# Prompt attention of a hybrid decoder step: TensorE makes a step's value products ahead of the step's transposes

## The reference

```
s = (q_nope @ k_nope^T + q_rope @ k_rope^T) * scale     # kind A
s = q @ k^T * scale                                      # kind B, + log of how many dilations hit the key
p = softmax(mask(s));   o = p @ v
```

## Time and profile before

| | |
|---|---|
| time, median of 3 runs | 1124.61 us (1124.18 to 1126.54) |
| profiled execution, span from first to last instruction | 1121.6 us (median less span: 3.0 us) |
| instructions | 21305 |
| TensorE busy | 98% of the span |
| DVE, ACT, POOL busy | 51%, 42%, 7% |
| stage with the change | about 229 to 333 us of the span |

### The profile page before, as it was taken

One profiled execution on the slowest core, in us unless ns is written; L12 is line 12 of the kernel. 1 busy time (PEld: TensorE's weight loads), 2 busy tenths in 40 slices (PEclk: granted clock), 3 DMA queues, 4 the chain that ended last, 5 costly groups with the idle time before them and its releaser, 6 DMA issues.

```text
span 1121.6 us, 21305 instructions
## 1 busy us (share of the span) xinstructions
PE 1100.4 (98%) x8216; PEld 947.9 (85%) x8216; DVE 572.8 (51%) x999; ACT 465.5 (42%) x812; POOL 81.9 (7%) x124
## 2 busy tenths in 40 slices
PE   9999999989989999999999999999999999999998
PEld 8897888645557777777776999999999999999998
DVE  4321444276657566666657994444423344444554
ACT  4334222355546656565566343333211232223421
POOL 5300011024000000000000220000000000000000
PEclk9999999988989999999999999999999999999999
DMA  7754541325957677788751245645724554562222
GB/s 292 244 190 170 207 141 57 105 113 185 328 171 269 191 246 250 252 270 268 243 180 62 96 150 185 227 151 182 264 88 141 188 206 159 196 221 79 89 87 92
DMA packets 68591, 202.79 MB, mean 181 GB/s; under 512 B 7426, under 2 KB 40195, under 8 KB 67235
## 3 DMA queue, kind: packets, MB, share of 16 engines
q1 hardware_dynamic: 66338, 131.89, 35.9%
q0 software_dynamic: 2176, 69.90, 17.6%
HBM read 196.67 MB, written 72.13 MB: 240 GB/s over the span
## 4 chain that ended last, share of the span: by engine, by line
PE 88%; DVE 5%; issue 3%; ACT 2%; POOL 1%; DMA 0%; SPq 0%; POOLq 0%; DVEq 0%
PE ps L549 52%; PE ps L1346 14%; PE ps L1449 4%; PE ps L1334 2%; PE ps L1323 2%; PE ps L1403 1%; PE ps L1378 1%; PE ps L1397 1%; PE ps L477 1%; PE ps L1308 1%; PE ps L1303 1%; PE ps L449 1%; PE ps L486 1%; POOL xs L726 1%; PE ps L1216 1%
## 5 line engine op out<-in xcount | busy, mean ns | idle before, releaser
L549 PE MATMUL ps<-aHi,wHi 128*128 128x272 f32 x1168 | 245.9, 292 | 0.3 <-DVE aLo L389 0.3
L549 PE MATMUL ps<-aHi,wLo 128*128 128x272 f32 x1168 | 241.6, 288 | 0.0
L549 PE MATMUL ps<-aLo,wHi 128*128 128x272 f32 x1168 | 240.9, 288 | 0.0
L423 ACT ACTIVATE wHi<-ring 128x1024 fp32r<-128x1024 f32 (+3 forms) x102 | 113.4, 1112 | 240.3 <-PE ps L549 213.3
L428 DVE TENSOR_TENSOR wLo<-ring,wHi 128x1024 fp32r<-128x1024 f32 (+3 forms) x102 | 141.1, 1383 | 140.2 <-ACT wHi L423 140.1
L549 PEld LDWEIGHTS ps<-aHi,wHi 128*128 128x128 f32 x1168 | 183.6, 188 | 8.8 <-issue 7.1
L549 PEld LDWEIGHTS ps<-aLo,wHi 128*128 128x128 f32 x1168 | 183.5, 188 | 0.0
L549 PEld LDWEIGHTS ps<-aHi,wLo 128*128 128x128 f32 x1168 | 182.5, 189 | 0.0
L1671 DVE TENSOR_REDUCE ssq<-att 128x8 f32<-128x512 f32 x128 | 87.2, 681 | 83.7 <-ACT att L916 83.7
L916 ACT ACTIVATE att<-ps 128x512 f32<-128x512 f32 x128 | 76.4, 597 | 104.7 <-PE ps L1346 104.1
L1346 PE MATMUL ps<-wkHi,pgHi 128*128 128x512 f32 x256 | 104.2, 407 | 1.5 <-DVE pgLo L1665 1.2
(11 more groups left out here) (266 smaller groups left out, 1476.2 us busy)
## 6 DMA issues: line engine op xcount, KB each, us to landing
out_o_cv<-in_cv POOLq DMA_DIRECT2D x16, 2044.0 KB, 9.1
ring<-in_wgu SPq DMA_DIRECT2D x44, 512.0 KB, 4.3
big<-in_pgt SPq DMA_DIRECT2D x128, 144.0 KB, 2.3
big<-in_pgl SPq DMA_DIRECT2D x128, 128.0 KB, 2.3
kv<-in_ck SPq DMA_DIRECT2D x8, 1792.0 KB, 10.4
ring<-in_win SPq DMA_DIRECT2D x21, 512.0 KB, 4.9
kv<-in_cv SPq DMA_DIRECT2D x8, 1024.0 KB, 5.6
kv<-in_cv SPq DMA_DIRECT2D x24, 256.0 KB, 6.1
```

The costliest lines, as they stand in the source:

```text
L423: nc.scalar.activation(wHi[:, u % 2, 0:width], ring[:, u % 2, 0:width], ACT.Copy).then_inc(w_hi, 1)
L549: ins = nc.tensor.matmul(pair[rows, a, 0:HT], w[:, c], xx[:, k, a * HT:(a + 1) * HT], start=(k == 0 and z == 0), stop=(k == nk - 1 and z = ...
```

## The change

In each step of TensorE's loop the block with the value products of unit n - 3 moves ahead of the block with the transposes of unit n - 2. No instruction is added, removed or changed, and every wait stays with its block. ACT's, DVE's, POOL's and SP's programs stay as they are.

```diff
                 if n < len(units):
                     ...  scores of unit n
-                if n >= LAG_T and n - LAG_T < len(units):
-                    m = n - LAG_T
-                    i = units[m][1]
-                    pe.wait_ge(a_p, m + 1)
-                    if m:
-                        pe.wait_ge(a_tc, m)
-                    for j in range(i + 1):
-                        for z in range(2):
-                            last = pe.transpose(ps[1][:, z, j * P:(j + 1) * P], probs_of(m, z)[:, j * P:(j + 1) * P], cm(C_ID))
-                    last.then_inc(a_t, 1)
                 if n >= LAG_PV:
                     m = n - LAG_PV
                     p, i = units[m]
                     pe.wait_ge(a_tc, m + 1)
                     ...  wait for a_o, value products
                     last.then_inc(a_pv, 1)
+                if n >= LAG_T and n - LAG_T < len(units):
+                    m = n - LAG_T
+                    i = units[m][1]
+                    pe.wait_ge(a_p, m + 1)
+                    if m:
+                        pe.wait_ge(a_tc, m)
+                    for j in range(i + 1):
+                        for z in range(2):
+                            last = pe.transpose(ps[1][:, z, j * P:(j + 1) * P], probs_of(m, z)[:, j * P:(j + 1) * P], cm(C_ID))
+                    last.then_inc(a_t, 1)
```

## The result

The changed kernel takes 1134.5 us (median of 4 executions, 1132.2 to 1137.6) against 1124.8 (median of 4); the ratio is 1.0086 (95% interval 1.0068 to 1.0104). A second round of 6 executions gave 1133.3 and a ratio of 1.0085 (1.0062 to 1.0108). Over all 10 the median is 1133.4; over 101 executions of the kernel before, made beside the experiments, it is 1124.3. So the change costs 9 to 10 us.

What follows compares the result with a forecast made beforehand. TensorE was taken to bound the kernel nearly throughout. Waits of 1.5 - 0.1 + 1.55 + 2.7 us, with 0 for ACT, DVE and the clock's change, gave +5.7 on 1124.6, so 1130.3 us; range 1126.3 to 1134.0.

Steps and rivals of the forecast that it cites:

- What bounds it, and the trade: TensorE bounds the kernel; T gets one PV more of cover against DVE, ACT's copy loses one PV of cover.
- The middle, the pauses, the start: Uncovered copies in steps 12-14, 20-22: +1.5 us; PV's output-copy waits in steps 7, 16, 31: +1.55; steps 4, 6: -0.1.
- The end: From step 32 on, without scores, each PV follows its own T and three copies are bare: +2.7 us, largest and surest term.
- The clock: Both half-clock falls in the stage stay; the first loss is kept at 4.7 us, the second's change taken as 0.
- the second stretch: Half-clocked time around 330 us, 6.8 us long, costing 2.7; change taken as 0, between 1.2 saved and 3 more.
- The span: Profiled span plus 3.0 us around it is the median of the runs, 1124.6 us, on which the sum stands.
- No effect: Rival: today's order might be as tied to ACT's copy as the new one; 1124.6 us, chance 0.04.
- faster: Rival: T's waits for DVE vanish while copies stay hidden; 1122.6 to 1123.0 us, chance 0.04.
- One fall less: Rival: the pauses shift and the clock's fall at 250 us stays out; 1125.6 us, chance 0.10.
- Another fall: Rival: new waits in threes bring the clock down once more, costing 4.7 us more; 1135.0 us, chance 0.08.
- a clock row of 0.5 where none was: Sign that the forecast is wrong: a half-clock row in the profile at a place that had none before.

Runs made afterwards that it cites:

- the run for it: Kernel before with the new order in steps 7 and 31 alone: 1126.6 us, ratio 1.0018 (1.0003 to 1.0034).
- the fitted fill of the changed kernel: Changed kernel with 2 dummy matrix products in step 7 and 3 in step 31, sized to fit the pauses: 1125.0 us, ratio 1.0012.

## Why the prediction was right and where it failed

**What bounds it, and the trade: right.** T's waits for DVE went, PV's for the copy came, at the units named. What is left over of the copy's way was measured at 0.48, 0.27 and 0.48 of idle time, and 0.69, 0.90 and 1.11 where the copy is bare. One small error is in it: the way was read from T's recorded end, the cover of S from start to start, so each wait was taken 0.07 too short. It makes 0.1 in each round and 0.2 at the end, and is most of why the waits came to 6.2 and not to 5.7.

**The middle, the pauses, the start: right in waits.** Step 7 has 2.39 (forecast 2.4), step 31 3.06 (3.1), step 16 0.81, step 6 0.48. Missed was 0.27 for the copy of unit 1 in step 4, but it costs nothing: T(2) starts 1.49 us behind S(4), as before (1.48), since it waits for DVE in any case. By runs the middle costs 2.8 (forecast 2.1) and the start 0.4 (-0.1), both within their intervals.

**The end: right in the trace, too large as a difference.** 0.69 + 0.90 + 1.11 = 2.7 came. But "PV(31) follows PV(30) with no gap" was read at half clock, where TensorE's own work is longer and covers more. At full clock the old end has 0.7 of such waits, so there the reordered end costs some 2.0.

**The clock: the step that failed.** It is the term at nothing: "In the second stretch the same work is now strewn with 2.7 us of waits ... I take 0 and keep both ends." The ends were -1.2 and +3. In the profile the stretch went on to 344 us, some 3 us into the next stage's products, and the work at half clock costs 3.4 more than before, a little over the upper end. In the medians the executions have 12.6 half-clocked us more, at 0.34 to 0.39 each +4.3 to +4.9. What the runs show in the term's place: the waits of the end take the second stretch from 3.4 to 6.8 us to 13.6 to 17.2, and alone bring about half of the 12.6 (+5.7 to +6.8). The other half is not located. The growth of the pauses may be part of it, but the run for it doesn't decide.

So the forecast of 5.7 is made up of 5.7 for the waits and 0 for the clock; the profile has 6.2 for the waits, and 3.4 less 1.0 for the clock. In the medians, 9.0 less the clock's share leaves 4.1 to 4.7 for the waits; this is a remainder and not a measurement of its own, and by means in place of medians it is 5.1 to 5.8.

**The stretches before.** The prediction has the clock fall twice in this stage. In the profile that it read it falls three times (3.4 us more at 225 us), and the 1.0 us that this costs is in the time before and not in any term. It is luck of that execution: of the eight profiles with a lag of 3, the late output copy and no dummy products, five have a stretch between 225 and 243 us.

**The span.** I read 3.0 us around the span. The executions listed here have 1.8. The profiled one was thus itself about a microsecond below the median, and its half-clocked time with it (20 us by its clock of 0.991).

**The rivals.** "No effect" and "faster" fell with the first waits in the trace. "One fall less" did not come at 250 us. "Another fall" is the nearest: its 1135.0 is half a microsecond from the measured 1134.5, and the forecast's own sign of being wrong, "a clock row of 0.5 where none was", came at 330 to 340 us. Its mechanism is not what happened, though: no new stretch began in the changed kernel's profile, an old one became 10 us longer. In one profile, the fitted fill of the changed kernel, the three bare copies of the end were followed by a stretch of some 3.4 us (clock 0.83 from 330 to 340 us) with nothing longer than the 1.11 and 1.22 us at 331 to 334 us ahead. That speaks for the rule of the Trainium skill (TensorE: Matmul & The Clock Gate, "A second HAM failure mode: psum-queue depth-cycling"), that short idles between groups can move the clock; the middle's rounds, three waits of 0.3 to 0.5 us among full work, did not in any of the seven profiles that have them. Why the clock falls in one execution and not in another stays open, and so do the stretches at 225 to 243, 295 and 610 us: the one near 295 us follows no wait of over 0.5 us, but the small products of `absorb` in step 24.

## What to carry to other kernels

When work is moved ahead of other work on one engine, ask what the second was covering: here the end of T's waits for DVE (1.0 us once, 0.5 twice) was bought with the cover of ACT's copy (0.3 to 1.1 us, eleven times). Price a wait on TensorE twice, by its length and by the half-clocked time that it brings or prolongs. Take the second from the spread of many executions rather than from the one that was profiled, and don't put it at nothing where waits are put into a stretch that is already at half clock. Before reordering the engine that is full, look at who answers it late: putting one small DVE copy at the head of its step gained 6 us, more than any order on TensorE, and with it the two orders took the same time.

## What the runs showed that was not expected

- Dummy products in two pauses made the kernel before 6.4 us faster (0.9947).
- The time of one and the same kernel is close to a line in its half-clocked time, 0.34 us for each microsecond over 101 executions, less than the 0.46 that a T at half clock loses. It fits with this that a part of the half-clocked time is waits, 3.9 of 17.2 us in the changed kernel's second stretch; no run separates it.
- A float32 product of 128x512 with all 128 rows takes 0.91 us. The scores, two products with 64 rows each, take 1.06 for both together.
